# A two-block transformer kernel in fp32: recurrence and differential attention as two stages, or as one

## The chip, the cores and the metric

The kernel runs on one core of a Trainium2 chip. The metric is the device time of one execution in microseconds (us). The engines have short names here: PE is the matrix engine (PEld its weight loads), DVE the vector engine, ACT the scalar engine, POOL the GpSimd engine, SP the engine whose queue issues the weight transfers. Each runs its own list of instructions in order; they meet only through semaphores.

## What is computed

A sequence of 512 tokens of width 1024 goes through a two-layer block and then through a one-layer block, all in fp32. Only the middle of the second block matters here. It projects the normalised and modulated input `u` to seven groups of 512 columns. Four feed a gated linear recurrence of 4 heads with 128 features each, three feed a differential attention of 4 heads, and both results go through one output matrix.

```python
proj = u @ w_in[l]                                  # 1024 -> 7 * 512
hq, hf, hi, hg, aq, ak, av = jnp.split(proj, offs, axis=-1)
# recurrence, each head: f = lb + (1 - lb) * sigmoid(hf); k = 1 - f; b = cumsum(log f)
#   A[t, s] = sum_k q[t, k] * k[s, k] * exp(b[t, k] - b[s, k])   for s <= t
#   o = A @ v;  o = rmsnorm(o) * silu(g)
# difference, each head: two causal softmaxes p0, p1 of scaled scores with a distance bias
#   w = p0 - lam * p1;  o = rmsnorm(w @ v) * 0.8
mix = jnp.concatenate([o_hg, o_da], axis=-1) @ w_out[l]
h = h + g1 * mix
```

## The kernel before

Everything is kept transposed: 128 features on the partitions, 512 tokens in the row. A weight matrix comes in **units** of 1024 x 128 (512 KB). SP loads a unit into one of the 4 slots of `raw`. ACT copies it, rounded, to `whi` (`split_hi`, L321), and DVE (for most of the recurrence POOL) writes the rest to `wlo` (`split_lo`, L332). `product` (L335) then issues 24 matmuls of 128 x 512: eight slices of the contraction, each as high x high, high x low and low x high (L347 to L349). Splits are made two units ahead of the unit in use. PSUM has eight banks of 128 x 512. Each stage below uses banks 6 and 7 for products and banks 0 to 5 for the rest.

**Stage "recur"** handles the 4 heads of the recurrence, 4 units each (q, f, i, g: `recur_g`). A head's decay sums are made by a scan (L1606) of logarithms. The score matrix of a head is split into dyadic **levels**, with blocks of 64, 32, ... 1 tokens: in each, the second half of a block attends to the first half. For a level, DVE subtracts a reference column (L1629), ACT takes the absolute value and then the exponential of its negative (L1342, L1344) over 512 columns, DVE multiplies it with the keys into `klev` (L1655) and POOL with the queries into `qlev` (L1163). Only two buffers (`elev`) hold such exponentials, so a subtraction waits for both products two levels back. PE forms the level's four 128 x 128 products (L1936), and DVE picks the level's entries out of PSUM into `amat` by a mask, four 128-column instructions for each level (L1667). Chunks further apart go through `kch`, `qch` (L1945). PE multiplies `amat` with the values (L1954), and the head's norm follows: a square on ACT, a sum over features on PE (L1043), a logarithm and an exponential on ACT (L1033, L1035), three refining steps on DVE (L1053 to L1058), a scale, a gate, and the split into `oh` and `ol` (L1039, L1075).

**Stage "diff"** follows with 3 units for each head. PE makes two score triangles of 1280 columns (L897), DVE adds the bias and takes the row maxima (L982), ACT exponentiates and sums (L957), POOL scales the second triangle (L1020), DVE mixes both (L1012), PE transposes the mix (L915), ACT copies it (L966), PE multiplies it with the values (L930), and the same head norm follows.

**Stage "mix"** is `res_pe` over 8 units of the output matrix. After it come the feed-forward layer and the end.

The order on each engine is written out by hand. `woven` and `normed` say for the two stages which part of head t stands before which part of head t+1: on PE the products of head t+1 stand between the transposes of head t and its level or flip matmuls. The tiles of the two stages lie in the same memory, so the second starts when the first is done with them.

## Time and profile before

| | us |
|---|---|
| median of 3 runs | 2090.36 (2089.86 to 2091.28) |
| the profiled execution | 2090.5 |
| its span, first to last instruction | 2088.7 |
| PE busy in the span | 1942.4 (93%) |
| DVE busy | 1192.1 (57%) |
| ACT busy | 820.3 (39%) |
| POOL busy | 217.5 (10%) |

"Busy" of PE counts a matmul as busy for its whole duration, although the next one begins before it ends. So the share says that PE seldom stood idle, and not that it ran at its peak. Times inside the span are counted from its first instruction.

### The profile page before, as it was taken

How to read it: one execution, taken by the hardware profiler on the slowest of the kernel's cores; microseconds unless marked ns; L12 is line 12 of the kernel's file. 1: busy time of each engine (PE TensorE's matmuls, PEld its weight loads, DVE VectorE, ACT ScalarE, POOL GpSimd, SP SyncE). 2: the span in 40 equal slices, each digit the busy share in tenths (PEclk: the TensorE clock that was granted, in tenths of full speed). 3: DMA queues.
4: the chain of work that ended last, by engine and by line, in shares of the span. 5: the costliest groups of instructions: out<-in, count | busy, mean ns of one | idle time of the engine just before them, and what ended most of it. 6: DMA issues, size and time to landing. Idle time of an engine off the chain costs nothing.

```text
span 2088.7 us, 25136 instructions
## 1 busy us (share of the span) xinstructions
PE 1942.4 (93%) x8986; PEld 1558.0 (75%) x8986; DVE 1192.1 (57%) x1635; ACT 820.3 (39%) x1100; POOL 217.5 (10%) x188
## 2 busy tenths in 40 slices
PE   7999999999999999999999997977489679999998
PEld 6777778888887777778888775766366458888886
DVE  4344454444798766554444788787756554444322
ACT  6555543232223444444444222444224334444322
POOL 0000010000111000010000122355312110000000
PEclk9999999999999999999999999998699889999998
DMA  3111132233454332132323454111021123233331
GB/s 128 61 60 60 40 105 95 92 100 98 159 180 162 98 98 86 59 103 94 97 91 98 163 179 158 61 41 41 21 81 61 33 68 101 85 97 99 94 91 69
DMA packets 56297, 193.59 MB, mean 93 GB/s; under 512 B 7088, under 2 KB 7600, under 8 KB 56112
## 3 DMA queue, kind: packets, MB, share of 16 engines
q1 hardware_dynamic: 47712, 163.60, 24.0%
q0 software_dynamic: 7520, 27.79, 4.1%
q10 hardware_dynamic: 1008, 1.45, 0.2%
q8 instruction: 35, 0.57, 0.1%
q14 instruction: 22, 0.18, 0.0%
HBM read 186.52 MB, written 2.10 MB: 90 GB/s over the span
## 4 chain that ended last, share of the span: by engine, by line
PE 73%; DVE 12%; issue 8%; ACT 4%; POOL 1%; DMA 1%; DVEq 0%; ACTq 0%; POOLq 0%
PE ps L347 21%; PE ps L349 21%; PE ps L348 21%; DVE wlo L332 2%; DVE tmps L774 2%; DVE wada L774 1%; PE ps L897 1%; DVE tmps L778 1%; PE ps L1812 1%; PE ps L915 1%; POOL qlev L1163 1%; PE ps L1817 1%; PE ps L1793 1%; PE ps L1936 1%; PE ps L1829 1%
## 5 line engine op out<-in xcount | busy, mean ns | idle before, releaser
L347 PE MATMUL ps<-xh,whi 128*128 128x512 f32 x1536 | 607.7, 396 | 28.7 <-DVE xl L877 17.1
L349 PE MATMUL ps<-xh,wlo 128*128 128x512 f32 x1536 | 601.4, 392 | 0.0
L348 PE MATMUL ps<-xl,whi 128*128 128x512 f32 x1536 | 601.2, 391 | 0.0
L332 DVE TENSOR_TENSOR wlo<-raw,whi 128x1024 fp32r<-128x1024 f32 (+1 forms) x292 | 360.9, 1244 | 207.2 <-ACT whi L321 201.7
L321 ACT ACTIVATE whi<-raw 128x1024 fp32r<-128x1024 f32 (+1 forms) x304 | 310.5, 1037 | 226.9 <-PE ps L349 226.3
L347 PEld LDWEIGHTS ps<-xh,whi 128*128 128x128 f32 x1536 | 290.2, 189 | 100.0 <-issue 24.2
L349 PEld LDWEIGHTS ps<-xh,wlo 128*128 128x128 f32 x1536 | 290.4, 189 | 61.5
L348 PEld LDWEIGHTS ps<-xl,whi 128*128 128x128 f32 x1536 | 290.6, 189 | 59.4 <-issue 0.7
L347 PE MATMUL ps<-acth,whi 128*128 128x512 f32 x528 | 213.0, 403 | 0.2
L349 PE MATMUL ps<-acth,wlo 128*128 128x512 f32 x528 | 208.5, 395 | 0.0
L348 PE MATMUL ps<-actl,whi 128*128 128x512 f32 x528 | 208.2, 394 | 0.0
L723 ACT ACTIVATE tmps<-tmps 128x512 f32<-128x512 f32 x66 | 41.8, 633 | 306.8 <-DVE tmps L739 207.3
L444 POOL TENSOR_TENSOR sqsum<-sqsum,tmps 128x512 f32<-128x512 f32 x39 | 52.1, 1336 | 939.3 <-ACT tmps L414 939.3
L349 PEld LDWEIGHTS ps<-acth,wlo 128*128 128x128 f32 x528 | 99.4, 188 | 23.3
L347 PEld LDWEIGHTS ps<-acth,whi 128*128 128x128 f32 x528 | 99.6, 189 | 21.6 <-issue 0.6
L348 PEld LDWEIGHTS ps<-actl,whi 128*128 128x128 f32 x528 | 99.6, 189 | 21.3 <-issue 0.2
L739 DVE TENSOR_TENSOR tmps<-ps,rstd 128x512 f32<-128x512 f32 x44 | 30.4, 692 | 133.2 <-PE ps L349 133.2
L749 DVE TENSOR_TENSOR actl<-tmps,acth 128x512 f32 (+1 forms) x66 | 45.7, 693 | 65.0 <-ACT acth L725 65.0
L347 PE MATMUL ps<-oh,whi 128*128 128x512 f32 x192 | 76.6, 399 | 4.6 <-DVE ol L1075 1.6
L1936 PE MATMUL ps<-qlev,klev 128*128 128x128 f32 x224 | 38.9, 349 | 41.3 <-DVE amat L1667 20.5
L348 PE MATMUL ps<-ol,whi 128*128 128x512 f32 x192 | 75.8, 395 | 0.0
L349 PE MATMUL ps<-oh,wlo 128*128 128x512 f32 x192 | 75.8, 395 | 0.0
(284 smaller groups left out, 2366.5 us busy)
## 6 DMA issues: line engine op xcount, KB each, us to landing
raw<-in_gu SPq DMA_DIRECT2D x132, 512.0 KB, 3.3
raw<-in_down SPq DMA_DIRECT2D x48, 512.0 KB, 4.0
raw<-in_qkv SPq DMA_DIRECT2D x24, 512.0 KB, 4.3
wada<-in_ada POOLq DMA_DIRECT2D x24, 512.0 KB, 3.8
tmps<-in_ada POOLq DMA_DIRECT2D x24, 512.0 KB, 3.6
raw<-in_qkvb SPq DMA_DIRECT2D x24, 512.0 KB, 3.7
raw<-in_down SPq DMA_DIRECT2D x24, 384.0 KB, 3.2
raw<-in_recur SPq DMA_DIRECT2D x16, 512.0 KB, 3.4
```

Source lines behind the costliest of these rows:

```text
L321: act.activation(whi[:, s, 0:n], raw[:, s, 0:n], ACT.Copy).then_inc(hi_done, 1)
L332: eng.tensor_tensor(wlo[:, s, 0:n], raw[:, s, 0:n], whi[:, s, 0:n].bitcast(F32), ALU.subtract).then_inc(lo_done, 1)
L347: pe.matmul(ps[:, bank], whi[:, s, w], hi[:, k0 + k], start=start and k == 0, stop=False)
L348: pe.matmul(ps[:, bank], whi[:, s, w], lo[:, k0 + k], start=False, stop=False)
L349: mm = pe.matmul(ps[:, bank], wlo[:, s, w], hi[:, k0 + k], start=False, stop=stop and k == n - 1)
L444: pool.tensor_tensor(sqsum[:, :], sqsum[:, :], sq[m % 2][:, :], ALU.add).then_inc(r.added.sem, 1)
L723: act.activation(tmp[i][:, :], tmp[i][:, :], ACT.Silu).then_inc(f.silu.sem, 1)
L739: dve.tensor_tensor(tmp[i][:, :], ps[:, 2 * i], rstd[:, :], ALU.mult).then_inc(f.gate.sem, 1)
L749: dve.tensor_tensor(actl[:, 2 * t + i], tmp[2 + i][:, :], acth[:, 2 * t + i].bitcast(F32), ALU.subtract).then_inc(f.lo.sem, 1)
L774: dve.tensor_tensor(w.rearrange("p (k c) -> p k c", k=KT), w.rearrange("p (k c) -> p k c", k=KT), csil.unsqueeze(2).to_broadcast((P, KT, P ...
L778: dve.reduce_sum(ada_part[par], w.rearrange("p (k c) -> p c k", k=KT), AX_X).then_inc(ada_sum, 1)
L1936: mm = pe.matmul(ps[:, n % 4, w], k[:, w], q[:, w], start=True, stop=True, skip_group_check=True)
```

## The change

The two stages "recur" and "diff" become one stage, "duo". Its 28 units stand in one list: for head t+1 the units f, q, i, g (recurrence) and v, d (values and queries of the difference), with k, the difference's keys of head t, behind f. All four engines run a written-out loop over t = -1 ... 3. In round t they work on the levels and the difference of head t and on the products and decays of head t+1. Further parts of it:

- The seven `qlev` and seven `klev` tiles, the two `elev` and `kch` become one tile `levels` of 8 x 512 columns, worked on in place. For a level, key columns and query columns are exponentiated each with its own sign and then multiplied, as two instructions of 256 columns in strided views instead of two or three of 512. The absolute value goes away; both multiplications are on DVE.
- DVE's reciprocal in the gate becomes a logarithm and an exponential on ACT and two refining steps on DVE.
- The masked picks of a level are one instruction of 512 columns instead of four of 128. `amat` keeps only the diagonal chunks, is cleared once, and the chunks further apart are copied by ACT into `crossb`.
- Products and results leave PSUM by ACT. All `split_lo` and the scaling of the second triangle are on DVE. POOL keeps `qch`, one instruction for each head.
- The biases are loaded head by head into two tiles. The output product ("mix") starts its first four units early, in the last round.

```diff
+DUO = [(kind, 0) for kind in "fqigvd"]
+for _t in range(HG - 1):
+    DUO += [("f", _t + 1), ("k", _t)] + [(kind, _t + 1) for kind in "qigvd"]
+DUO.append(("k", HG - 1))
+BANK_OF = {"f": 7, "q": 6, "i": 7, "g": 6, "v": 7, "d": 6, "k": 6}
...
+            for t in range(HG):
+                pool.wait_ge(duo_out, UNIT_OF["q", t] + 1)
+                pool.wait_ge(rc.exp, 9 * t + 1)
+                wait(pool, rc.cross, t)
+                pool.tensor_tensor(qch, hq[:, :], elog_d, ALU.mult).then_inc(rc.qch, 1)
...
+            def gate_inverse(t):
+                act.wait_ge(rc.gate, 4 * t + 1)
...
+                act.activation(elog_d, cum, ACT.Ln).then_inc(rc.inverse, 1)
+                act.wait_ge(rc.inverse, 2 * t + 1)
+                act.activation(elog_d, elog_d, ACT.Exp, scale=-1.0).then_inc(rc.inverse, 1)
...
+                act.wait_ge(rc.diff, 8 * t + (n + 1))
+                key, query = halves(levels[:, n], LEVELS[n - 1])
+                act.activation(key, key, ACT.Exp, scale=-1.0)
+                act.activation(query, query, ACT.Exp).then_inc(rc.exp, 1)
...
+                if t >= 0:
+                    head_hi(2 * t, t)
+                if more:
+                    high("g", n)
+                    wait(act, hn.scaled, 2 * n - 3)
+                    unit_out("g", n, ACT.Silu, hgate[n % 2][:, :])
+                    act.preload_act_table_set(EXP_LN)
+                    token_out(2 * n, 4, vtok2)
+                if t >= 0:
+                    act.wait_ge(df.flipped, t + 1)
+                    act.activation(dprob[1][:, :], tri_ps[0], ACT.Copy).then_inc(df.flat, 1)
...
+                    dve.copy_predicated(amat[:, :, :], levmask[:, n:n + 1, :].broadcast_to([P, NB, P]),
+                                        ps[:, n % 4].rearrange("p (a b) -> p a b", b=P)).then_inc(rc.pick, 1)
...
+                    for part, source in zip(halves(levels[:, n], LEVELS[n - 1]), (hk, hq)):
+                        ins = dve.tensor_tensor(part, part, halves(source[:, :], LEVELS[n - 1])[source is hq], ALU.mult)
+                    ins.then_inc(rc.lev, 1)
...
+            for t in range(-1, HG):
+                n = t + 1
+                more = n < HG
+                if t >= 0:
+                    level_scores(t)
+                    cross_scores(t)
+                if more:
+                    dense("f", n)
+                if t >= 0:
+                    dense("k", t)
+                    recur_values(t)
+                    scores(t)
+                if more:
+                    dense("q", n)
                 else:
...
+                    mix_early(0)
+                if t >= 0:
+                    pe.wait_ge(df.masked, 8 * t + 1)
+                    head_sum(2 * t, 3)
...
+                if more:
+                    dense("i", n)
+                    dense("g", n)
...
+                    turn_values("i", n, 4)
...
+                if t >= 0:
+                    flips(t)
+                if more:
+                    dense("v", n)
...
+                if t >= 0:
+                    diff_values(t)
+                if more:
+                    dense("d", n)
...
+                    turn_values("v", n, 5)
...
+                    head_sum(2 * t + 1, 4)
```

Where the instructions stand is shown at three places. First PE, at the matmuls of a head's values in the recurrence: `vtok_136` holds the values, `wada` the squares to be summed, `tmps` the next head's values to be transposed. Before:

```order
L1954 MATMUL ps<-amat,vtok_136 128x512
L1954 MATMUL ps<-amat,vtok_136 128x384
L1954 MATMUL ps<-amat,vtok_136 128x256
L1954 MATMUL ps<-amat,vtok_136 128x128
L1087 UNCONDITIONAL_BRANCH
L1087 ISA
L1043 MATMUL ps<-wada,ones 128x512
L1917 ISA
L1921 MATMUL ps<-ident,tmps 128x128 x4
```

and now, with the score matmuls of the difference (`kd`, `qd`) and a product (L358) right behind:

```order
L2007 MATMUL ps<-amat,vtok_123 128x128
L2020 MATMUL ps<-kd,qd 128x512 x2
L2020 MATMUL ps<-kd,qd 128x384 x2
L2020 MATMUL ps<-kd,qd 128x128 x2
L2020 MATMUL ps<-kd,qd 128x256 x2
L358 MATMUL ps<-xh,whi 128x512
```

The sum of the squares (L1043 before, L2053 now) has moved from right behind the values to behind that product. Second ACT, in the middle of a round, around the copy of the transposed mix (L966 before, L1349 now). Before, in "diff" (L321 is a split, `onew` and `var` belong to the head's norm, `dprob_146` to the next head's score triangle):

```order
L321 ACTIVATE whi<-raw 128x1024
L966 ACTIVATE dprobt<-ps 128x1280
L1103 REGISTER_ALU
L1103 COMPARE_AND_BRANCH
L1031 ACTIVATE onew<-oraw 128x512
L1033 ACTIVATE tmps<-var 128x512
L1035 ACTIVATE tmps<-tmps 128x512
L957 ACTIVATE dprob_146,small<-dprob_146,small 128x512
```

and now:

```order
L1240 ACTIVATE oh<-tmps 128x512
L332 ACTIVATE whi<-raw 128x1024
L1221 ACT_TABLE_LOAD
L1221 ACTIVATE hgate_119<-ps 128x512
L1345 ACT_TABLE_LOAD
L1246 ACTIVATE vtok_123<-ps 128x512
L1349 ACTIVATE dprob_129<-ps 128x1280
L1273 ACTIVATE levels<-levels 128x32x8
L1274 ACTIVATE levels<-levels 128x32x8
```

The copy has moved behind the head's `oh` copy, a split, the gate and two table loads. Third DVE, between the mix of a head and the scale of a norm. Before:

```order
L1012 SCALAR_TENSOR_TENSOR dprob_145<-dprob_145,small,dprob_146 128x128
L1694 COPY kd<-ps 128x512
L1027 COPY oraw<-ps 128x512
L1103 REGISTER_ALU
L1103 COMPARE_AND_BRANCH
L1707 COPY bias_now<-alibi 128x512
L1047 TENSOR_SCALAR var<-ps 128x512
```

and now:

```order
L1712 SCALAR_TENSOR_TENSOR dprob_128<-dprob_128,small,dprob_129 128x128
L343 TENSOR_TENSOR wlo<-raw,whi 128x1024
L1654 TENSOR_TENSOR levels<-levels,hk 128x512
L1657 TENSOR_SCALAR kch_120<-levels,tmps 128x128 x2
L1661 TENSOR_SCALAR kch_121<-kch_120,tmps 128x128
L1648 TENSOR_TENSOR levels<-tmps 128x512 x2
L1578 TENSOR_TENSOR var<-var,tmps 128x512
L1580 SCALAR_TENSOR_TENSOR var<-var,tmps 128x512
L1582 SCALAR_TENSOR_TENSOR var<-var,tmps 128x512
L1591 SCALAR_TENSOR_TENSOR oraw<-oraw,vec,var 128x512
```

A split, the far chunks (`kch`) and two subtractions of the next head now stand between the mix and the norm of the recurrence's head; before, no work of the recurrence stood there. ACT's `oh` copy of the recurrence's head (L1240) waits for the scale behind these.

## Rows read from the trace of the kernel before

**Rows 1.** Windows of "recur", "diff", "mix": length, engines' busy time, clock, DMA.

```profile
1302.70:1523.10 220.40, 158.93 (x744) 130.12 (x744) 170.51 (x292) 90.16 (x129) 91.85 (x56) 0.87 0.12 39
1523.10:1646.50 123.40, 99.54 (x449) 74.32 (x450) 68.98 (x157) 47.07 (x100) 21.13 (x18) 0.93 0.18 60
1646.50:1693.60 47.10, 45.05 (x193) 35.65 (x191) 26.66 (x30) 13.94 (x18) 9.09 (x7) 1.00 0.26 82
```

**Rows 2.** Waits of PE in "recur": us in total, times, longest.

```profile
PE ps L1936 <- DVE amat L1667: 20.5, 4, 5.2
PE ps L1936 <- POOL qlev L1163: 19.0, 2, 18.2
...
PE ps L347 <- DVE var L1047: 7.3, 3, 3.2
PE ps L1043 <- ACT wada L1031: 6.1, 4, 1.5
```

**Rows 3.** Timeline of PE: start, duration, instruction; matmuls overlap the next.

```profile
1302.70 0.77 PE L347 MATMUL ps<-xh,whi 128*128 128x512 f32 x1 [7.65 <-DVE xl L877]
...
1315.06 0.39 PE L347 MATMUL ps<-xh,whi 128*128 128x512 f32 x1
...
1318.45 0.39 PE L347 MATMUL ps<-xh,whi 128*128 128x512 f32 x1
...
1353.01 3.74 PE L1936 MATMUL ps<-qlev,klev 128*128 128x128 f32 x32
...
1692.75 0.40 PE L349 MATMUL ps<-oh,wlo 128*128 128x512 f32 x1
```

**Rows 4.** The chain that ended last, start and duration of pieces in it.

```profile
1367.04 1.35 PE ps L1945 x12
...
1369.65 2.41 PE ps L1954 x8
...
1560.61 1.11 PE ps L915 x10
1561.74 1.25 ACT dprobt L966
...
1566.96 1.13 PE ps L1043 x2
1568.08 2.36 PE ps L897 x16
```

**Rows 5.** Groups in 1299 to 1700: shape, count, busy us, mean ns, idle before.

```profile
L1629 DVE TENSOR_TENSOR tmps<-tmps 128x512 f32<-128x512 f32 x32 | 37.0, 1158 | 11.2 <-POOL qlev L1163 9.4 <-DVE tmps L1606 0.6
L1667 DVE COPY_PREDICATED amat<-levmask,ps 128x128 f32<-128x128 uint8 x128 | 28.6, 297 | 5.1 <-DVE amat L1667 3.0 <-PE ps L1936 1.7
L1591 DVE RECIPROCAL tmps<-tmps 128x512 f32<-128x512 f32 x4 | 13.4, 3353 | 0.1
...
L1053 DVE TENSOR_TENSOR var<-var,tmps 128x512 f32<-128x512 f32 x8 | 5.5, 693 | 4.4 <-ACT tmps L1035 4.3
...
L1344 ACT ACTIVATE tmps<-tmps 128x512 f32<-128x512 f32 x32 | 20.2, 632 | 1.0
```

**Rows 6.** Timeline of ACT around the gate's function, then of DVE in "diff".

```profile
1329.53 0.60 ACT L1317 ACTIVATE sqsum<-ps 128x512 f32<-128x512 f32 x1 [3.02 <-PE ps L349]
1330.15 1.28 ACT L1318 ACT_TABLE_LOAD   x1
1331.44 1.06 ACT L321 ACTIVATE whi<-raw 128x1024 fp32r<-128x1024 f32 x1
...
1583.15 1.22 DVE L332 TENSOR_TENSOR wlo<-raw,whi 128x1024 fp32r<-128x1024 f32 x1
1584.28 1.94 DVE L1012 SCALAR_TENSOR_TENSOR dprob<-dprob,small,dprob 128x512 f32<-128x512 f32 x4
```

**Rows 7.** A window with PE alone: length, busy, clock, DMA; then a timeline row inside.

```profile
1428.00:1432.00 4.00, 3.51 (x10) 0.70 0.00 0
...
1428.49 0.49 PE L347 MATMUL ps<-xh,whi 128*128 128x512 f32 x1 [3.24 <-DVE var L1047]
```

More of the change, by code:

```diff
@@ L268, in load_units @@
             for u in phases:
+                if u.name == "duo":
+                    for j, (kind, t) in enumerate(DUO):
+                        array, place_in = SOURCE[kind]
+                        wait(sp, lo_done, u.number(0, j) - 2)
+                        sp.dma_start(raw[:, u.slot(j), :], a[array][t * (4 if array == "recur" else 3) + place_in, :, :])\
+                          .then_inc(landed[u.slot(j)], 16)
+                    continue
                 def one(t, j):
@@ L688, in body @@
                     if early and leading(t):
-                        rest = (KT - 1,) if j < 2 else None
-                        product(pe, u, t, j, EARLY[j], hi, lo, start=rest is None, ready=ready if first else None,
+                        rest = REST_PART if j < early else None
+                        product(pe, u, t, j, banks[j], hi, lo, start=rest is None, ready=ready if first else None,
                                 part=rest)
@@ L894, in a_ @@
                     w = (c + 1) * P
-                    for i in (1, 0) if two else (0, 1):
+                    for i in range(2):
                         rows = slice(64 * i, 64 * i + 64)
@@ L899, in a_ @@
                           .then_inc(s.scored, 1)
[L900 to L903 removed]
+                wait(pe, s.lo, t)
                 for b in range(NB):
@@ L908, in b_ @@
             def b_(t):
-                for i in range(1 if two else 2):
-                    pe.wait_ge(s.mixed if two else s.scaled, 4 * t * (1 if two else 2) + (4 * i + 4))
+                for i in range(2):
+                    pe.wait_ge(s.scaled, 8 * t + (4 * i + 4))
                     for c in range(NB):
@@ L1985, in diff_c @@
[L1985 to L1995 removed]
+                mm.then_inc(rc.cross, 1)
@@ L1996, in _ @@
+            pe.wait_ge(hn.copied, 2 * HG)
+            mix_early(3)
+            for j in range(4):
+                mix_early(j, (3,))
+            res_pe(pe, U["mix"], r2a, oh, ol, mixed, early=4, banks=EARLY_MIX)
             ffn_pe(pe, U["gu2"], f2, n_lo["2"])
```

985 lines of the change are left out of this document (503 added, 482 removed).

## The prediction

> **What bounds the kernel now.** I read the windows of the three stages first, then the waits of PE in them, then its timeline for the pace of each kind of matmul. The change touches only the stretch from the first product of "recur" at 1302.7 to the last matmul of "mix", which begins at 1692.75 and lasts 0.40: 390.5 us [rows 3]. The rest of the program is the same. In that stretch no engine is full. "Mix" runs PE without holes; "diff" nearly does; in "recur" PE is busy for 158.9 of 220.4 us, at a mean granted clock of 0.87 [rows 1]. So the loss is in "recur". Its waits name it: 20.5 us in four for the picks, 19.0 in two for `qlev` from POOL (the long one, 18.2, in the last head, which has no products left to put beside it), 7.3 in three before products and 6.1 in four before the sum over a head's features [rows 2]. Each is a piece of one head's chain between ACT, DVE and POOL with nothing on PE beside it. DVE is the next full engine there (170.5 us), and part of that is slow work rather than much work: the subtraction of 512 columns takes 1158 ns on average, while an ordinary one of that size (L1053) takes 693 [rows 5].
>
> **The pace of PE.** From 1315.06 to 1318.45 five slices of a product begin, 0.68 us a slice, so a unit of eight slices is 5.44 us [rows 3]. The first 16 level matmuls (each recorded as two) take 3.74 [rows 3], so eight levels are 7.5. The far chunks take 1.35, each product with the values 2.41 (I use it for both kinds), the flips 1.1, the scores 2.4; a sum over features takes 1.1 from a standing start, and I book 1.0; four transposes of values I book at 0.6, from ten flips in 1.1 with some for the start [rows 4]. One round of the new loop is then 7 units, 38.1; levels 7.5; far chunks 1.35; two value products 4.8; scores 2.4; flips 1.1; two turns 1.2; two sums 2.0. **That is 58.4 us of PE work for a head of each kind.** For "mix" I keep 5.6 a unit: PE was busy for 45.05 us with its 8 [rows 1].
>
> **What the other engines have to do in a round.** DVE was busy for 170.5 + 69.0 = 239.5 us in the two stages [rows 1]. Out go the reciprocals (13.4 [rows 5]), and 15 by the subtractions at 0.69 instead of 1.158. The picks were 28.6 [rows 5]; as 32 instructions at the 0.69 of other 512-column work they are 22, and at worst what they are now, 0.9 for a level; nothing excludes less, down to a third below 0.69, but it would gain nothing where PE sets the pace. Copies go to ACT or away, 28 of 512 columns at 0.69 and 16 narrower or simpler ones, together about 26. In come 12 splits at 1.22 that POOL did (14.6; one is shown in rows 6), the scaling of the second triangle (near the 1.94 of the mix of the same columns [rows 6], so at most 8), and four times two refining steps of the gate (5.6 at 0.69). The 28 `klev` products become 56 halves of 256 columns, for keys and queries. The trace has no such half; between half of 0.69 and the whole of it I take 0.42, nearer to the half, since an instruction's fixed part does not halve: 24 us against 19 for 28 wholes. The sum is about 211 us, 53 for each head, and the other slowed instructions beside POOL would take it lower. ACT was busy for 90.2 + 47.1 = 137.3 [rows 1]; the 32 absolute values go (20 us at 0.63, the price of the exponentials of rows 5), 56 halves at 0.42 stand in place of 28 wholes at 0.63 (6 more), and some 44 copies, gate steps and far-chunk copies come (28). That makes about 151, 38 a head. So PE, at 58.4, is the bound, with 6 us of room on DVE and 20 on ACT. POOL, busy for 91.9 us in "recur", keeps one product for each head, which the far chunks need a whole round later: nothing. The transfers stay the same 28 units of 512 KB, and a DMA share of 0.12 to 0.26 leaves room [rows 1].
>
> **What the order lets through.** All queues are in order, so room is not enough. I walked one round, with durations from the rows and 0.08 of overlap between two instructions of DVE or ACT where the second does not need the first (four parts of the mix take 1.94 in all [rows 6]). Count from the first level matmul. PE: levels and far chunks until 8.8, f until 14.3, k until 19.7, values and scores until 24.5, q, sum, i and g until 41.8, turn and flips until 43.5, v until 49.0. The picks stay right behind the levels, even at 0.9. The next head's gate needs f (14.3) and passes ACT and DVE twice, so the scan ends at 24.2 and its subtractions at 25.5; peaks and exponentials of the two triangles end at 34.2, the mix at 36.3, well before the flips need it at 42.4. Behind the mix DVE has a split, the far chunks, two subtractions, and then the norm: scaled at 43.6. **ACT waits for that scale until 43.6**, and behind it in its queue stand a copy of 0.6, a split of 1.06, the gate with two table loads of 1.28, the values' copy, and only then the copy of the flipped mix, 1.25 [rows 4, 6]. It ends at 50.0, and the product with the values, ready at 49.0, begins at 50.2. So a round is 58.4 + 1.2 = **59.6 us**. The last level's factors are ready on DVE at 58.4, 7 us before PE comes to them.
>
> **The start.** The first product takes 9.5 us as now, since it waits for its input. DVE is free only at about 1315.6, after the residual's root, and its queue has the gate, the scan and two subtractions ahead of the split of unit g: PE waits 3.5 us for that. The first levels begin 41.0 after 1302.7, against 50.3 before (1353.0 [rows 3]). **The end.** Round 3 has no next head. Levels, far chunks, k, values and scores end at 19.0; three early units of "mix", six slices of eight each, fill part of the softmax's chain, but the flips wait 3.4 us for the mix, the last sum 1.0 for its square, and the fifth unit of "mix" 2.7 for its split, which stands behind two residual sums on DVE. Round 3 with "mix" takes 69.5 of work and 7 of waits, 76.3 with rounding. Sum: 41.0 + 3 x 59.6 + 76.3 = 296.1 against 390.5, a gain of 94.4.
>
> **The clock.** After an idle 3.24 us, matmuls of 0.23 went to 0.43 apart for a while; the window from 1428 shows a granted clock of 0.70, a mix of both levels, 2.4 and 1.2 GHz [rows 7]. That lost about 1.6 us (eight matmuls by 0.2). Three waits of that size remain, at the start and in the end, so I take off 4. The gain is 90, and 2090.5 of the profiled execution less 90.4 is **2000 us**. Its time and the median before differ by 0.14, so the same number serves for both. The waits of 1.2 in the middle are like the many of that size in "diff", whose clock in mid-stage I take to be full.
>
> **A rule weighed.** Between the gate's function (0.60 from 1329.53) and the next instruction stands a table load of 1.28 and nothing else: the split begins at 1331.44, 0.01 after the load [rows 6]. So each switch costs ACT 1.28. The Trainium skill (ScalarE: Activation LUTs, What ACT_TABLE_LOAD costs) adds about 1.38 us of draining to each load. This place of the trace shows no such gap, but in the new loop both loads stand in the one path that PE waits for; its price is among the rivals.
>
> **Rivals.**
> *PE never waits* (chance 0.1). If the waits at g, in the rounds and at the end all vanish, 3.5 + 3.6 + 7 + 4 of the clock come back: 2000 - 18, but the chain from scores to mix in round 3 is real, so 1986.
> *The handover is slower than walked* (0.2). If instructions of one engine don't overlap, and halves cost a whole, the scale comes 2 us later, the loads and copies 2 more; the wait for the flipped mix becomes 5, as the picks' waits do now (5.2 longest [rows 2]), and draws the low clock with it. That is 3 x (3.9 + 1.6), plus 4 at the ends: 2020. In its favour: four instructions of ACT in a row behind one wait.
> *The loads drain* (0.04). Two loads by another 1.4 each in every round would put the wait at 4 us: 3 x 2.8 = 8, so 2008. The page's rule above is this rival; rows 6 speak against it.
> *Slower* (0.04). The halves are strided, down to every second column, and the picks read a mask that is repeated four times. If such views run far below one column a cycle, DVE becomes the bound. It has 6 us of room, and the gain is gone when a round takes 59.6 + 22.6. Then 22 instructions a round must cost 30 us more than booked, 1.4 each; at 2.3 us for each of the 14 halves and 0.9 for each pick DVE has 53 + 28 us in a round, with 3 of waits 84, and the kernel takes 2000 + 4 x 24.4, about 2098. Against it: the subtractions already work on views down to two columns with a repeated one, and take 1.16 in the mean for 512 columns even with POOL beside them [rows 5].
> *The heads don't overlap* (0.02). If one wait of the 30 or so in a round closes a ring (the levels of the next head only behind the flips of this one, say), the round is as long as the two before, 77, and the time stays at 2090. I found none in the walk.
>
> **How the numbers follow.** The forecast has 0.6: 2000, with 1992 to 2012 of its own. The fast case and the slow handover hold 0.3, so the range goes from 1984 to 2024 and leaves out some 0.15. Faster by over 0.2% (about what a measurement of this kernel can tell from no change) is all but the last two: 0.94, of which I give 0.01 to accidents that cost more. Same 0.02, slower 0.05.
>
> **What would show it.** Right: PE over 95% busy in the new stage, rounds of 59 to 61 us between first level matmuls, a wait of about 1 us before the difference's value product named after the copy of the flipped mix, 3 to 4 us before the first g. Wrong: means above 0.6 for the halves or above 1.0 for the picks; DVE with no idle time and PE waiting before levels; waits of 5 us in each round with a granted clock near 0.9; first levels later than 1350.

## The result, and the profile after

The merged kernel takes **1998.75 us** in the median (1997.78 to 1999.41), the kernel before 2090.23 beside it: a ratio of 0.956 with a 95% interval of 0.9547 to 0.9574. The forecast was 2000.0 with a range of 1984 to 2024. The profiled execution took 1997.78, with a span of 1996.0 against 2088.7.

PE's busy time by rounds of the new stage, then over the whole stretch; the last row answers to [rows 1]. The columns are the window, its length, busy us (and instructions) of PE, PEld, DVE, ACT and POOL, the granted clock, the DMA share, GB/s.

```profile
1301.35:1342.51 41.16, 37.72 (x152) 28.66 (x153) 34.54 (x56) 25.50 (x43) 1.84 (x1) 0.93 0.21 66
1342.51:1401.52 59.01, 57.60 (x306) 47.20 (x305) 41.70 (x82) 33.18 (x66) 1.91 (x2) 1.00 0.21 71
1401.52:1461.02 59.50, 57.60 (x305) 47.20 (x304) 45.43 (x88) 34.16 (x68) 1.97 (x2) 1.00 0.20 67
1461.02:1522.58 61.56, 59.21 (x306) 47.91 (x305) 45.88 (x88) 34.42 (x68) 1.83 (x2) 0.97 0.20 65
1522.58:1600.99 78.41, 72.21 (x345) 57.77 (x343) 49.10 (x80) 27.82 (x50) 9.01 (x7) 0.96 0.17 54
1301.35:1600.99 299.64, 284.34 (x1408) 228.73 (x1408) 216.65 (x394) 155.09 (x291) 16.55 (x14) 0.97 0.20 64
```

The stretch went from 390.5 us to 299.6. PE stood idle for 15.3 us of it, against 87 before (390.5 less the 303.5 of [rows 1]), and it was busy for 19 us less with much the same matmuls (1386 records before, 1408 now), which fits a granted clock of 0.97 where "recur" had 0.87. So of the 91 us some 72 are holes that closed and 19 are clock. DVE is busy for 45 us of a round of 59; it is not the bound.

PE's waits from 1295 to 1620 (us in total, times, longest), which answer to [rows 2]:

```profile
PE ps L358 <- DVE xl L920: 15.5, 6, 7.2
PE ps L358 <- DVE wlo L343: 5.9, 2, 3.4
PE ps L2046 <- ACT dprob L1349: 5.7, 3, 2.4
PE ps L478 <- POOL sqsum L455: 3.0, 1, 3.0
PE ps L2037 <- DVE dprob L1712: 2.1, 1, 2.1
PE ps L2053 <- ACT tmps L1227: 0.7, 1, 0.7
```

In the stretch no wait for picks or for POOL is left; the one for POOL's squares follows "mix" and was there before (2.97). Of the first line 7.2 lie ahead of the stretch and 7.4 behind it, and only 1.0 in its first product. The second is unit g at the start (2.5) and the fifth unit of "mix" (3.4). The third is the one that the prediction named, the copy of the flipped mix, once in each of rounds 0 to 2. PE's timeline shows the rounds, and each of these waits in brackets at the matmul that ended it:

```profile
1342.51 6.42 PE L1972 MATMUL ps<-levels 128*128 128x128 f32 x56
...
1392.49 2.42 PE L2046 MATMUL ps<-dprob,vtok 128*128 128x512 f32 x8 [1.41 <-ACT dprob L1349]
1401.52 6.41 PE L1972 MATMUL ps<-levels 128*128 128x128 f32 x56
...
1451.99 2.42 PE L2046 MATMUL ps<-dprob,vtok 128*128 128x512 f32 x8 [1.90 <-ACT dprob L1349]
1461.02 6.41 PE L1972 MATMUL ps<-levels 128*128 128x128 f32 x56
...
1511.94 4.04 PE L2046 MATMUL ps<-dprob,vtok 128*128 128x512 f32 x8 [2.35 <-ACT dprob L1349]
1522.58 6.41 PE L1972 MATMUL ps<-levels 128*128 128x128 f32 x56
```

Rounds of 59.01, 59.50 and 61.56. Behind the first two waits the eight products with the values take 2.42, behind the third 4.04: there PE was for most of 4 us at its lower level (1.2 GHz; a granted clock of 0.60), as a window of PE alone shows beside the one a round earlier:

```profile
1452.00:1456.00 4.00, 4.00 (x16) 1.00 0.00 0
1512.00:1516.00 4.00, 4.00 (x9) 0.60 0.02 4
```

The groups that answer to [rows 5] (count, then busy us and mean ns, then idle time before):

```profile
L1611 DVE COPY_PREDICATED amat<-levmask,ps 128x512 f32<-128x512 uint8 x32 | 23.5, 733 | 5.7 <-PE ps L1972 5.2
L1648 DVE TENSOR_TENSOR levels<-tmps 128x512 f32<-128x512 f32 x32 | 21.7, 718 | 0.1
L1670 DVE TENSOR_TENSOR levels<-levels,hk 128x256 f32<-128x256 f32 x28 | 11.8, 420 | 5.8 <-ACT levels L1274 5.8
...
L1273 ACT ACTIVATE levels<-levels 128x256 f32<-128x256 f32 x28 | 11.7, 419 | 0.4 <-DVE levels L1648 0.4
...
L1701 DVE TENSOR_SCALAR dprob<-dprob,small 128x384 f32<-128x384 f32 x4 | 4.2, 1052 | 0.0
```

A pick of 512 columns costs 733 ns, a strided half 420 ns on DVE and 419 on ACT, and the subtraction fell from 1158 to 718. The last group stands out: 384 columns of a scaling by one number cost 1052 ns in the mean of four. It comes back below.

### The profile page after: what moved, and what is told of

It is laid out like the page before. It is cut to its first block, busy times and chain, and to the rows that moved or that the text cites. A ratio compares the mean times of both kernels' runs of the same rounds, so it can differ in the third digit from the quotient of the medians.

```text
span 1996.0 us, 24683 instructions
## 1 busy us (share of the span) xinstructions
PE 1920.5 (96%) x9010; PEld 1544.0 (77%) x9010; DVE 1142.2 (57%) x1551; ACT 823.7 (41%) x1144; POOL 113.0 (6%) x124
## 4 chain that ended last, share of the span: by engine, by line
PE 76%; DVE 12%; issue 6%; ACT 4%; DMA 1%; DVEq 0%; ACTq 0%; SPq 0%; POOL 0%
PE ps L358 22%; PE ps L360 22%; PE ps L359 22%; DVE wlo L343 2%; DVE tmps L817 2%; DVE wada L817 2%; DVE tmps L821 1%; PE ps L1972 1%; PE ps L1858 1%; ACT whi L332 1%; PE ps L939 1%; PE ps L1863 1%; PE ps L1839 1%; PE ps L1875 1%; PE ps L964 1%
## 5 line engine op out<-in xcount | busy, mean ns | idle before, releaser
L358 PE MATMUL ps<-xh,whi 128*128 128x512 f32 x1536 | 608.8, 396 | 23.3 <-DVE xl L920 16.0
L343 DVE TENSOR_TENSOR wlo<-raw,whi 128x1024 fp32r<-128x1024 f32 (+1 forms) x304 | 375.1, 1242 | 216.5 <-ACT whi L332 211.0
L358 PEld LDWEIGHTS ps<-xh,whi 128*128 128x128 f32 x1536 | 289.8, 189 | 94.1 <-issue 17.9
L360 PEld LDWEIGHTS ps<-xh,wlo 128*128 128x128 f32 x1536 | 289.7, 189 | 61.6
L359 PEld LDWEIGHTS ps<-xl,whi 128*128 128x128 f32 x1536 | 290.2, 189 | 59.5 <-issue 1.4
L358 PE MATMUL ps<-acth,whi 128*128 128x512 f32 x528 | 213.0, 403 | 0.2
L358 PEld LDWEIGHTS ps<-acth,whi 128*128 128x128 f32 x528 | 99.6, 189 | 21.5 <-issue 0.6
L358 PE MATMUL ps<-oh,whi 128*128 128x512 f32 x192 | 78.1, 407 | 6.4 <-DVE wlo L343 3.4
L768 ACT ACTIVATE acth<-tmps 128x512 f32 x66 | 41.7, 632 | 66.6 <-DVE tmps L790 66.6
```

The source lines that it names most:

```text
L343: eng.tensor_tensor(wlo[:, s, 0:n], raw[:, s, 0:n], whi[:, s, 0:n].bitcast(F32), ALU.subtract).then_inc(lo_done, 1)
L358: pe.matmul(ps[:, bank], whi[:, s, w], hi[:, k0 + k], start=start and k == 0, stop=False)
L359: pe.matmul(ps[:, bank], whi[:, s, w], lo[:, k0 + k], start=False, stop=False)
L360: mm = pe.matmul(ps[:, bank], wlo[:, s, w], hi[:, k0 + k], start=False, stop=stop and k == n - 1)
L768: act.activation(acth[:, 2 * t + i], tmp[2 + i][:, :], ACT.Copy).then_inc(f.hi.sem, 1)
```

## The experiments

For each kernel the stretch is measured from its first product to the sum of the squares behind "mix", from the starts of PE's rows; a round is from one head's first level matmul to the next head's. These are free of what lies ahead of the stretch, which differs by up to 3.3 us from one profiled execution to the next (the stretch began at 1302.7 before, between 1299.4 and 1301.7 in all the others). Each ratio is to the kernel before measured beside that kernel; its medians were 2089.03 to 2090.23.

| kernel | median us | 95% interval of the ratio | stretch | start | rounds | to the sum |
|---|---|---|---|---|---|---|
| before | 2090.23 | | 393.4 | 50.3 | | |
| after | 1998.75 | 0.9547 to 0.9574 | 302.6 | 41.2 | 59.0, 59.5, 61.6 | 81.4 |
| e1_serial | 2033.25 | 0.9713 to 0.9743 | 338.8 | 41.2 | 72.2, 72.0, 71.8 | 81.7 |
| e8_serial_old | 2033.94 | 0.9719 to 0.9751 | 339.0 | 41.8 | 72.0, 71.9, 71.8 | 81.6 |
| e2_old_ops | 2000.89 | 0.9556 to 0.9585 | 308.7 | 43.4 | 61.3, 61.3, 61.3 | 81.5 |
| e4_before_dve | 2082.41 | 0.9954 to 0.9982 | 388.4 | 49.9 | | |
| e5_qch_dve | 1994.97 | 0.9528 to 0.9554 | 301.4 | 42.8 | 59.0, 59.0, 59.0 | 81.6 |
| e6_load_slack | 1998.50 | 0.9551 to 0.9583 | 302.7 | 41.2 | 59.0, 59.6, 61.6 | 81.4 |
| e7_load_chain | 2013.68 | 0.9617 to 0.9649 | 318.3 | 42.8 | 64.2, 64.9, 65.1 | 81.4 |
| e3_flat_first | 1990.04 | 0.9506 to 0.9532 | 296.2 | 42.8 | 57.3, 57.3, 57.3 | 81.5 |
| e9_best | 1989.33 | 0.9507 to 0.9533 | 294.7 | 42.8 | 57.3, 57.3, 57.3 | 80.0 |
| e10_best | 1989.57 | 0.9509 to 0.9535 | 293.8 | 42.8 | 57.3, 57.3, 57.3 | 79.1 |
| e11_no_pool_edit | 1987.59 | 0.9498 to 0.9524 | 293.6 | 41.2 | 57.3, 57.3, 57.3 | 80.5 |

### Which part of the change brings the gain

**No overlap of two heads.** The new stage, but head t+1's products, decays and splits stand behind everything of head t, on all engines.

```diff
-    DUO += [("f", _t + 1), ("k", _t)] + [(kind, _t + 1) for kind in "qigvd"]
+    DUO += [("k", _t), ("f", _t + 1)] + [(kind, _t + 1) for kind in "qigvd"]
...
-            for t in range(-1, HG):
+            for t, half in [(t, half) for t in range(-1, HG) for half in (0, 1)]:
-                more = n < HG
+                more = n < HG and half == 1
...
-                if t >= 0:
+                if half == 0 and t >= 0:
```

> The changed kernel with the same instructions, but in each round all work of head t stands first on every engine and all work of head t+1 behind it; unit k comes before unit f. Theory (the gain is the overlap): the part of head t alone takes 19 us of matmuls to the scores, then PE waits for the softmax chain, some 36 us to the last sum; the products of head t+1 with their chain take 38 as in the first round. 74 to 78 us a round against 59.6, three rounds: +45 to +55, so 2045 to 2055. Rival (the gain is the lighter work on the levels): the instructions are the same, so at most 2010.

It took 2033.25, between the two. PE's waits:

```profile
PE ps L2038 <- DVE dprob L1712: 22.4, 4, 6.8
...
PE ps L2047 <- ACT dprob L1349: 8.7, 3, 2.9
PE ps L358 <- DVE wlo L343: 5.9, 2, 3.4
PE ps L2054 <- ACT oraw L1228: 4.7, 4, 1.2
```

Three of these belong to the difference: the mix, its copy, the square. The line with `wlo` is again unit g and the fifth unit of "mix". **None belongs to the levels of the recurrence**, whose picks and factors held PE up before [rows 2]. A head's levels are made beside the products of the same head, of which there are now six in a row (f, q, i, g, v, d) where "recur" had four units. So the merged stage closes the holes of "recur" without any overlap of heads: 393.4 to 338.8, 54.6 us. The overlap of heads brings the other 36.2, the waits of the softmax chain and the low clock behind them.

The 54.6 hold more than the holes of "recur". "Diff" had holes too, and the longest of them, before the flips of the last head, had nothing beside it:

```profile
PE ps L915 <- DVE dprob L1012: 10.8, 1, 10.8
```

With the early units of "mix" in its place PE waits 2.07 there, and from there to the first of the later units 6.7 in all against 15.2 before. No kernel leaves these early units out, so their share, by these waits some 8.5 us, is an estimate. My 2045 to 2055 was worked out from rounds of 74 to 78; they take 72: 57.3 of work, 10.9 of waits, 4 of restarts and low clock (0.91 from 1340.98 to 1413.15).

**The old operations in the new order.**

```diff
-                act.activation(key, key, ACT.Exp, scale=-1.0)
-                act.activation(query, query, ACT.Exp).then_inc(rc.exp, 1)
+                act.activation(levels[:, n], levels[:, n], ACT.Abs).then_inc(absed, 1)
+                act.wait_ge(absed, 7 * t + n)
+                act.activation(levels[:, n], levels[:, n], ACT.Exp, scale=-1.0).then_inc(rc.exp, 1)
...
-                    dve.copy_predicated(amat[:, :, :], levmask[:, n:n + 1, :].broadcast_to([P, NB, P]),
-                                        ps[:, n % 4].rearrange("p (a b) -> p a b", b=P)).then_inc(rc.pick, 1)
+                    for c in range(NB):
+                        ins = dve.copy_predicated(amat[:, c, :], levmask[:, n, :], ps[:, n % 4, c * P:(c + 1) * P])
+                    ins.then_inc(rc.pick, 1)
...
+                dve.reciprocal(cum, cum).then_inc(rc.gate, 1)
```

> The changed kernel with three of the heavier forms back: absolute value and exponential over 512 columns for each level, the reciprocal of the gate on DVE, four picks of 128 columns for each level. Theory (overlap, PE sets the pace): picks and most level work lie where DVE and ACT have room; the reciprocal (3.35 us) replaces 0.65 + 0.65 + 0.7 + 0.75 and two handovers on the chain that ends in the flipped mix, so 0.5 to 1.5 us a round: 2000 to 2005. Rival (the lighter forms gave the gain): these were 15 us or more of each head before, so 2030 or more.

2000.89, inside the theory's range. These three lighter forms save DVE 10 us and ACT 8 from 1300 to 1606, and the kernel 2 in the medians. The profiled execution, with 2003.74 the longest of its four, has 6 more in the stretch. Most of the 6 is not the instructions' length: the wait for the flipped mix is 1.98 in each round, and behind each of the three the clock falls, as here, and so it does behind unit g.

```profile
1456.00:1460.00 4.00, 4.00 (x11) 0.60 0.00 0
```

**Both: no overlap, and the old operations.** If the lighter operations mattered where the other head gives no cover, this is where it would show.

> The kernel in which no head overlaps the next (2033), with the operations of before put back in it: absolute value and one exponential of 512 columns for a level, the reciprocal on DVE, four picks of 128 columns. It tells what of the 57 us that are gained without overlap of heads is due to lighter operations. Theory: little; a head's decays run beside its own five products there too, the last factors are ready some 5 us before their matmuls, and the operations add 3.5 us on ACT and 1.4 on the picks: 2033 to 2040. Rival: without the other head beside them the lighter operations are what is gained; ACT's 20 us, the picks' 5 and the reciprocals' 13 come back at least by half: 2052 or more.

2033.94 against 2033.25, with the same rounds of 72. The rival falls by 18 us. So these three forms are not what the change gains without overlap. Two other parts of it stay in this kernel and were not taken out of it: POOL has left the levels and the splits, which the next experiment weighs in the old order, and "mix" starts early. What is left of the 54.6 goes to the order by argument.

**The kernel before without POOL in the levels.**

```diff
-                    pool.tensor_tensor(qlev[n][:, :], hq[:, :], elev[n % 2][:, :], ALU.mult).then_inc(rc["qlev"], 1)
...
                     dve.tensor_tensor(klev[n][:, :], hk[:, :], elev[n % 2][:, :], ALU.mult).then_inc(rc["klev"], 1)
+                    dve.tensor_tensor(qlev[n][:, :], hq[:, :], elev[n % 2][:, :], ALU.mult).then_inc(rc["qlev"], 1)
```

> The kernel before with one thing changed: the seven query products of the levels and the product for the far chunks of each head (32 instructions) are done by DVE instead of POOL, in the same tiles. Theory: POOL's part in the recurrence costs in two ways, the waits for its product (19.0 us, 18.2 of it in the last head, where some 5 stay as DVE has to do them) and DVE's slower instructions beside it (subtractions 1158 ns instead of some 700, 15 us); against it stand 32 by 0.69, 22 us, on DVE, which is full only in part: 2072 to 2084, with subtractions under 850 ns. Rival: POOL takes work from an engine that is the bound there, and moving it to DVE costs the 22 us in the chain that PE waits for: 2095 or more.

2082.41, 7 us below the 2089.03 measured beside it: inside the theory's range, but not for its main reason.

```profile
PE ps L1936 <- DVE amat L1666: 18.7, 4, 5.0
PE ps L1936 <- DVE qlev L1654: 17.7, 2, 17.2
...
L1624 DVE TENSOR_TENSOR tmps<-tmps 128x512 f32<-128x512 f32 x32 | 28.5, 892 | 1.5 <-DVE tmps L1601 0.6
```

The wait in the last head went from 18.2 to 17.2, not to 5. It carried POOL's name [rows 2] because POOL came last; the chain of gate, scan and factors behind it is nearly as long with DVE in POOL's place. What POOL also cost was speed: the subtractions fell from 1158 to 892 ns (the splits are still on POOL), 8.5 us in 32. Which of the waits the 7 us come from is not separated further; 5.0 of them lie in the stretch (393.4 to 388.4).

### What PE waits for in a round

**Five multiplications more on DVE, beside the chain and in it.** Both kernels have this, from 0 to 2:

```diff
+            def burden():
+                for _ in range(5):
+                    if spares[0]:
+                        dve.wait_ge(spared, spares[0])
+                    spares[0] += 1
+                    dve.tensor_tensor(spare[:, :], rstd[:, :], rstd[:, :], ALU.mult).then_inc(spared, 1)
```

In one it stands ahead of the last level's factors:

```diff
                     low("d", n)
+                    if t >= 0:
+                        burden()
                     level(n, (7,))
```

> The merged kernel with five more multiplications of 512 columns on DVE, each dependent on the one before (about 3.6 us in all at the 0.69 to 0.72 of its own rows), in rounds 0 to 2, ahead of the last level's factors; their result is not used. Theory: PE waits for one chain alone in a round, from the gate by the scan, the mix and the scale to the copy of the flipped mix; the last level's factors are ready some 7 us before PE comes to them, so 3.6 us there cost nothing: 1997 to 2001. Rival: DVE as a whole sets the pace beside PE, and whatever is added to it shows: three rounds by 3.6, 2008 to 2011.

In the other ahead of the norm's last steps:

```diff
+                    if more:
+                        burden()
                     head_rest(2 * t)
                     head_scale(2 * t, t)
```

> The same five multiplications in the same rounds 0 to 2, but on DVE ahead of the last steps of the recurrence's norm, so in the chain to the copy of the flipped mix; their result is not used. Theory: each of the three waits before the difference's product with the values grows by 3.6, from 1.4, 1.9 and 2.4 to 5.0 to 6.0, that is 10.8 us, and the low clock comes with each of the first two as well: 2010 to 2015. Rival: the instructions stand in DVE's idle time (83 us in the new stretch), 1997 to 2002.

1998.50 and 2013.68: the same 11 us of DVE work cost nothing at one place and 15 at the other. The waits of the second (the first kernel has 5.7, 3, 2.4, as the kernel without any load):

```profile
PE ps L2058 <- ACT dprob L1351: 16.2, 3, 5.9
```

16.2 against 5.7 is 10.5 for 10.8 put in. The rest of the 15.7 that the stretch grew by (302.6 to 318.3) is clock: each of the three waits, 4.9, 5.4 and 5.9, now draws the lower level, and so did the one at the start. So at least 3.6 us were free at the first place. The step "the last level's factors are ready 7 us early" holds in the trace of the merged kernel: they are ready at 1400.23, 1459.73 and 1519.98, which is 6.7, 6.7 and 8.0 us before PE comes to them.

**The copy of the flipped mix ahead of the gate and its table loads.**

```diff
                 if t >= 0:
                     head_hi(2 * t, t)
+                    act.wait_ge(df.flipped, t + 1)
+                    act.activation(dprob[1][:, :], tri_ps[0], ACT.Copy).then_inc(df.flat, 1)
                 if more:
                     high("g", n)
...
-                if t >= 0:
-                    act.wait_ge(df.flipped, t + 1)
-                    act.activation(dprob[1][:, :], tri_ps[0], ACT.Copy).then_inc(df.flat, 1)
```

> The changed kernel with ACT's copy of the flipped mix moved ahead of the split, the gate and the two table loads. Theory (that queue is what PE waits for before the difference's value product): the waits of 1.41, 1.90 and 2.35 us go, and with the third the stretch at a clock of 0.60 behind it, about 1.6 us: 1991 to 1993. Rival (the wait comes from DVE's chain ahead of the scale, or the gate is late next): within 2 us of the changed kernel.

1990.04, 8.7 less, a little more than the theory gave. PE's waits name no `dprob` of ACT any more, and three rounds are exactly alike: 57.32. That is the work of a round, measured. What stood in the way can be seen in ACT's timeline of the kernel after, at the second of the waits:

```profile
1445.40 0.63 ACT L1240 ACTIVATE oh<-tmps 128x512 fp32r<-128x512 f32 x1 [6.22 <-DVE tmps L1595]
1445.94 1.04 ACT L332 ACTIVATE whi<-raw 128x1024 fp32r<-128x1024 f32 x1
1447.00 1.28 ACT L1221 ACT_TABLE_LOAD   x1
1448.29 0.60 ACT L1221 ACTIVATE hgate<-ps 128x512 f32<-128x512 f32 x1
1448.91 1.28 ACT L1345 ACT_TABLE_LOAD   x1
1450.21 0.60 ACT L1246 ACTIVATE vtok<-ps 128x512 f32<-128x512 f32 x1
1450.70 1.23 ACT L1349 ACTIVATE dprob<-ps 128x1280 f32<-128x1280 f32 x1
```

ACT stood idle for 6.22 us before the scale came, and from then to the copy, 5.3 us, it did other work. Its loads take 1.28 each, with 0.01 or 0.02 around them. The Trainium skill (ScalarE: Activation LUTs, What ACT_TABLE_LOAD costs) adds a draining of about 1.38 to each load; the trace doesn't show it in the new place either.

**The far chunks' product on DVE instead of POOL.**

```diff
-                pool.tensor_tensor(qch, hq[:, :], elog_d, ALU.mult).then_inc(rc.qch, 1)
...
                 if more:
+                    dve.wait_ge(duo_out, UNIT_OF["q", n] + 1)
+                    dve.wait_ge(rc.exp, 9 * n + 1)
+                    wait(dve, rc.cross, n)
+                    dve.tensor_tensor(qch, hq[:, :], elog_d, ALU.mult).then_inc(rc.qch, 1)
                     level(n, (1, 2))
```

> The changed kernel with the one product that POOL had for each head (the queries for the far chunks) on DVE, behind the scale of the norm. Theory (POOL beside it is what makes DVE's scaling of the second triangle slow, 1052 ns for 384 columns in place of about 0.4): the four scalings take 1.6 us instead of 2.32, the mix comes 0.7 earlier and with it the scale, so PE's wait shrinks by 0.7 a round, about 2 us: 1996 to 1997.5. Rival (that form is slow of itself): the four scalings stay at 2.3 us and the time at 1998 to 2000.

1994.97, a little better than the theory. The scaling of the second triangle and PE's waits there:

```profile
L1697 DVE TENSOR_SCALAR dprob<-dprob,small 128x384 f32<-128x384 f32 x4 | 1.7, 414 | 0.0
...
PE ps L2046 <- ACT dprob L1345: 4.2, 3, 1.4
```

With POOL idle the 384 columns take 414 ns instead of 1052, and the 128 columns 280 (L1697) instead of 539. But the 1052 and the 539 are means over unlike cases. In the kernel after, one scaling in each of rounds 0 to 2 was held up, here in rounds 0 and 2, and all the others took what they take here:

```profile
L1701 DVE TENSOR_SCALAR dprob<-dprob,small 128x128 f32<-128x128 f32 x1 | 1.3, 1327 | 0.0
...
L1701 DVE TENSOR_SCALAR dprob<-dprob,small 128x384 f32<-128x384 f32 x1 | 1.9, 1922 | 0.0
```

In round 1 it was one of 1460 ns. POOL's product beside it takes 1.37, and in round 2 POOL clears a tile right behind it (0.53), so the held one lasts about as long as POOL works. The four scalings take 2.32, 2.32 and 2.78 instead of 1.27: the one instruction that the change leaves to POOL costs DVE 1.05, 1.05 and 1.51 us in rounds 0 to 2, and nothing in round 3, where POOL has none.

Not all of this reaches PE, for without it the mix waits for ACT's exponentials, in rounds 1 and 2 for 0.46:

```profile
1435.27 0.18 DVE L1703 RECIPROCAL small<-small 128x4 f32<-128x4 f32 x1 [0.46 <-ACT dprob L1278]
```

Counted from the first level matmul of its round, the mix begins at 34.07 in all three rounds here, and at 34.07, 34.56 and 35.01 in the kernel after. So PE's waits are 1.41, 1.40, 1.40 instead of 1.41, 1.90, 2.35, the third no longer draws the low clock, and the third round is 59.0 instead of 61.6. Against this stand 0.7 a head on DVE, which has room. Of the 3.8 between the medians the rounds explain 3.0. In the profiled executions the stretch is only 1.2 shorter, since here the clock fell behind unit g (a start of 42.8 against 41.2).

### Putting it together

**Three edits.** Copy early, product on DVE, and the split of the fifth unit of "mix" ahead of the squares of the first two:

```diff
+                if begun == 2 and leading(t):
+                    split_hi(act, u, (1, 0), freed=3)
                 for j in range(u.body):
-                    if not leading(t) or j >= begun:
+                    if not leading(t) or j >= begun + (begun == 2):
                         split_hi(act, u, ahead(u, t, j, end))
```

and likewise `split_lo` on DVE.

> The merged kernel with three edits: the copy of the flipped mix ahead of the gate and its table loads, the product for the far chunks on DVE instead of POOL, and the split of the fifth unit of the output product ahead of the squares and the sums of the first two. Theory: the first two are not to be added, since both work on the same wait, which the first removes whole (1990.0); the third removes the 3.4 us of wait before the fifth unit and 1 of low clock behind it: 1984.5 to 1987. Rival: each engine's time counts, and the gains add up (8.7, 3.8 and 4.4 from 1998.8): 1981 to 1983.

1989.33: both fail. That the first two don't add up is right (rounds of 57.32, as with the first alone). But the third brought nothing: the stretch is 1.5 shorter only because the clock did not fall behind the flips this time (1.00 from 1548 to 1552, where the kernel with the early copy alone had 0.73). Two waits took the place of the one removed:

```profile
PE ps L478 <- POOL sqsum L455: 4.5, 1, 4.5
...
PE ps L358 <- DVE h L698: 1.8, 1, 1.8
```

The split was ready, and now PE waited 1.8 us for the residual sum `h`, which stood behind the split on DVE; and at the end of "mix" it waited 4.5 for the squares instead of 3.0. DVE's timeline shows the ring behind it (a closed chain, each step waiting for the one before), one unit of "mix" from split to split:

```profile
1586.34 1.48 DVE L343 TENSOR_TENSOR wlo<-raw,whi 128x1024 fp32r<-128x1024 f32 x1 [1.71 <-ACT whi L332]
1587.75 0.74 DVE L691 SCALAR_TENSOR_TENSOR h<-h,vec,rstd 128x512 f32<-128x512 f32 x1
1588.52 0.75 DVE L698 SCALAR_TENSOR_TENSOR h<-ps,mod,h 128x512 f32<-128x512 f32 x1
1590.98 1.47 DVE L343 TENSOR_TENSOR wlo<-raw,whi 128x1024 fp32r<-128x1024 f32 x1 [1.71 <-ACT whi L332]
```

4.64 us a unit: two steps on DVE, the square and the split on ACT, the split on DVE. PE, ahead of it, only waits longer at the end.

**The residual sum first, then the split.** The only difference is that DVE's `split_lo` stands behind the first unit's sum. A second kernel has POOL's product back as in the merged one.

```diff
                 for j in range(u.body):
+                    if begun == 2 and leading(t) and j == 1:
+                        split_lo(dve, u, (1, 0))
```

> The last kernel with one thing moved: DVE makes the residual sum of the first unit of the output product before the split of the fifth, not behind it; ACT still has the split ahead of the squares. Theory: behind the early units the ring of residual sum, square, split on ACT and split on DVE, 4.6 us a unit, runs behind PE and sets the end, so the 1.6 us won before the fifth unit came back as 1.5 before the sum of the squares; with the residual sums 1.9 earlier PE waits under 0.5 for the fifth unit and some 3.0 for the squares: 1985 to 1987. Rival: the last runs' 1989.3 is the level of what PE has to do, and nothing in the order moves it: 1988.5 to 1990.5.

> The same without the second of the three edits: the product for the far chunks is on POOL again. Theory: no wait of PE depends on it once the flipped mix is copied early, so this one is within 0.7 us of the one beside it: 1985 to 1987. Rival: DVE's slowed instructions beside POOL still cost PE something: 2 us or more above it.

1989.57 and 1987.59. Over the stretch the two are alike, 293.8 and 293.6, as the theory for the second has it. The medians are 2.0 apart, more than its 0.7; in the profiled executions, 1.7 apart, the difference lies ahead of the stretch, which began at 1301.66 in the one and at 1300.00 in the other. The rival of the second asked for 2 us or more in the other direction, so it falls. The first theory missed: PE waits 0.47 for the fifth unit as expected, but 1.27 for the sixth and 4.95 for the squares.

```profile
PE ps L478 <- POOL sqsum L455: 5.0, 1, 5.0
```

The ring started 0.9 us earlier than in e9_best, counted from the stretch's start, not 1.9. The missing one is this row, where the same step takes 0.74 in the other units; POOL's first addition of a square lay beside it, from 1565.61 for 1.80:

```profile
1566.18 1.78 DVE L691 SCALAR_TENSOR_TENSOR h<-h,vec,rstd 128x512 f32<-128x512 f32 x1
```

So PE runs ahead of the ring as before and waits at the end. Both kernels had one fall of the clock fewer than e3_flat_first (the first behind the flips, the second at the start), 1.6 each; without that the order of the split is worth some 1.0 of the 4.4 aimed at. e11_no_pool_edit is the fastest of all, and its five times (1986.56 to 1987.96) lie below all five of the early copy alone (1988.09 to 1991.67). But its interval (0.9498 to 0.9524) overlaps that of the early copy alone (0.9506 to 0.9532) by more than half. The early copy is what is shown to be worth having; what the other edits add is about as small as what can be told apart in the total.

## Why the prediction was right

**The bound** was named rightly: PE in the rounds, one chain that makes it wait once, and the chain is that of the walk (e7_load_chain beside e6_load_slack).

**What was lost before.** "So the loss is in 'recur'" was too narrow, and "diff" did not nearly run without holes: by [rows 1] PE was idle there for 23.9 of 123.4 us, 10.8 of them before the last head's flips. The forecast did not rest on it, since it added up the new loop from its own work and waits.

**The start.** 41.0 forecast, 41.16 measured, and here two errors cancel. Unit g waited 2.5, not 3.5, and the first product took 10.3, not 9.5.

**A round.** 59.6 forecast; 59.0, 59.5, 61.6 measured. Two terms were off in opposite directions, so the closeness of the number is partly luck. PE's work is 57.3 (e3_flat_first), not 58.4: a sum over features was booked at 1.0 and takes PE 0.56, as the next product begins that much behind it:

```profile
1562.72 1.13 PE L2053 MATMUL ps<-tmps,ones 128*128 128x512 f32 x2 [0.69 <-ACT tmps L1227]
1563.28 0.79 PE L358 MATMUL ps<-oh,whi 128*128 128x512 f32 x1
```

Two of these are 0.9 of the 1.1. And the wait was 1.4 to 2.4, not 1.2. The walk itself was close: PE comes to the product with the values at 48.6 in all three rounds (walked: 49.0), and the product begins at 50.0, 50.5 and 50.9 (walked: 50.2). That POOL's one product costs "nothing" was the step that failed: it holds DVE up by 1.05 to 1.51 us ahead of the mix, of which 0, 0.5 and 0.9 reach PE, and with the low clock the third round is 2.5 us longer. The clock in mid-stage was taken to be full; it was in two rounds of three.

**The end.** 76.3 forecast, 78.4 measured to the last matmul. The waits were 2.1, 0.7 and 3.4 (forecast 3.4, 1.0 and 2.7), 6.2 in all against 7.1. Two of them drew the low clock, which the prediction had in a term of its own.

**The other engines.** DVE was booked at about 211 us without "mix"; the whole stretch shows 216.7, and "mix" alone took 26.7 before. So it was booked some 20 us too high, on the safe side, as nothing waited for its total.

**The sum.** 296.1 and 4 for the clock were 300.1; 299.6 were measured. The low clock came three times, as forecast, but at one other place: in the third round instead of behind unit g. A further 1.35 lie ahead of the stretch, where the start varies by more than that between kernels.

**The rivals.** That PE never waits is what e3_flat_first makes of it in the rounds, not what the change does. The slower handover came by half a microsecond and a microsecond in two rounds, not by 3.9. The loads don't drain. Halves (420 and 419, booked 420) are far from the 2.3 us of the slower rival, and picks (733, booked 690) below its 0.9. PE waited for nothing of DVE's level work.

**The signs** came out close, not all inside: PE busy for 94.9% of the stretch (over 95% named), rounds of 59.0 to 61.6 (59 to 61), 1.4 to 2.4 before the value product (about 1), 2.5 before the first g (3 to 4).

**Of the parts of the change**, the prediction priced the lighter operations at nothing for PE, and that nearly holds (2 us in the medians, 6 with the falls of the clock in one profiled execution, and none without overlap). What it didn't ask is how the 90 divide between the merged stage and overlapped heads: 54.6 and 36.2. It looked for the gain in the walk of two heads; more than half came without a second head beside the first, mostly, as argued above, from longer cover for one.

## What to carry to other kernels

When a stage with a long chain on the other engines stands beside one that keeps PE busy, merge them before making the chain's instructions shorter: here the overlap of heads brought 36 us and putting the old forms back cost 2 to 6, while of the 55 that came without overlap a few belong to POOL's leaving the levels (5 in the old order) and to the early units of "mix" (some 8.5, an estimate). Then walk the one queue in which the critical result stands behind work that nobody waits for; moving one copy ahead of it brought 8.7 us. The engine named in a wait is the one that came last, not always the one that is too slow: taking POOL out of the 18.2 us wait left 17.2 of it.

## What the runs showed of the hardware

**POOL beside DVE.** While POOL multiplied two tiles of 512 columns (1.37 us), one DVE instruction of a row of short ones was held up: a scaling by one number of 128 columns took 1327 ns and one of 384 columns 1460, and 1922 where POOL cleared a tile right behind; without POOL they took 280 and 414. Their neighbours in the row took no longer than without POOL. The Trainium skill (GPSIMD Engine Reference, Key points) says that POOL shares its ways to the SBUF with DVE and contends with DVE instructions in a mode of two ports or with two inputs in the SBUF. The step of 1.78 us in e10_best has two such inputs, and the trace agrees there; in which mode the scalings ran no run here shows. A single POOL instruction can so cost where DVE's chain is the one that PE waits for.

**PE's clock after a wait.** After 1.41 and 1.90 us of idle time in a round of the merged kernel the granted clock stayed at 1.00; after 1.98 (three times in e2_old_ops), 2.35 (in the kernel after) and 4.9 to 5.9 (in e7_load_chain) it fell to between 0.54 and 0.62 over the next 4 us, at a cost of 1.6 to 1.9. It is no fixed function of the wait. In e4_before_dve it stayed at 1.00 after 2.17 us, in the window from 1416 to 1420. And after nearly the same wait at unit g, 2.47 in the kernel after and 2.49 in e3_flat_first, the clock stayed in the one and fell in the other, first after, then e3_flat_first, in windows of PE alone:

```profile
1324.00:1328.00 4.00, 2.83 (x13) 1.00 0.39 131
```

```profile
1324.00:1328.00 4.00, 3.64 (x10) 0.61 0.41 131
```

The wait of 2.07 at the last flips went both ways too. This is why the starts in the table are 41.2 or 42.8, and nothing between, for kernels with the same operations. What decides it stays open.
